# PEER experts of a hybrid decoder step: sample rows gathered like the row blocks, second products summed over four keys

## The chip, the cores and the metric

One core of a Trainium2 chip runs the whole step as one program. The metric is the device time of one execution in microseconds (us); lower is better. The engines are named as in the profile: PE (TensorE matmuls), PEld (its weight loads), DVE (VectorE), ACT (ScalarE), POOL (GpSimd, which issues the indirect DMAs) and SP (the engine that issues most other DMAs).

## The reference, cut to what matters

The step has 1024 prompt rows and 64 sample rows of width 1024. After the mixer sublayer every row goes through PEER: eight heads pick 16 of 16384 experts each, so a row has 128 picks, each with a gate. An expert is a pair of rows (two keys name it) in `expert_u` and `expert_v`.

```python
def block(tb):
    ...
    experts = e1 * N_KEYS + e2
    gate = jax.nn.softmax(top_s, axis=-1)
    ue = expert_u[experts]
    act = jax.nn.gelu(jnp.einsum('thkd,td->thk', ue, tb).astype(F32), approximate=False) * gate
    return jnp.einsum('thk,thkd->td', act.astype(tb.dtype), expert_v[experts])
```

The result is added to the residual, and a final RMSNorm follows.

## The kernel before, in words

The stages follow one another: input projection, SSD heads, RWKV heads, output projection (`output_projection`), picking (`pick_experts`), the spreading of gates (`spread_gates`), and the experts (`run_experts`, line 2787). The change leaves the first three as they are, but for the columns of `mixed` to which they store.

1088 rows are kept. They are split in two parts that are treated differently in `run_experts`:

- **Dense rows**: `DENSE = KEPT - BLOCKS * P` = 704 (the 64 samples and 640 prompt rows), as columns of `h` and `u`. For them all 16384 experts are computed, and the gate, zero for experts not picked, weighs the result. `spread_gates` turns picks into a gate table in DRAM, 64 rows (a group) at a time, each group in 8 batches of 8 rows: 11 groups, 88 batches.
- **Row blocks**: `BLOCKS = 3` blocks of 128 prompt rows, rows on partitions. For pick j of block b an indirect DMA on POOL fetches 128 rows of 4 KB (512 KB) of the first table (`fetch_u`), DVE forms a dot with `rows.u` (`dot_row`, line 3110), ACT takes Gelu of six dots at once, DVE weighs them (`weigh`, line 3115), a second indirect DMA fetches the rows of the second table (`fetch_v`) and DVE adds them with their weight to `rows.h` (`add_row`, line 3123).

`run_experts` goes over 64 periods. In each, g, the dense part handles two values of one key (`SET = 2`). PE makes the first products (`up_products`: 2 keys x 2 chunks of 352 columns x 8 x 3, for every product in full precision is three fp32r matmuls, lines 113 to 115, on a rounded part and a rest) and the second products of the period before (`down_products`: 8 tiles m x 2 chunks x 2 keys x 3): 192 matmuls. ACT rounds weights and activations and takes Gelu; DVE makes the rests (`rest`, line 3086: four of 1024 columns, two of 704), multiplies with the gates (line 3101, two of 704) and adds each of the eight tiles m from PSUM to `h` (`add_units`, line 3129, 704 columns). SP loads two `up` and two `down` weight tiles of 512 KB and 704 KB of gates. Beside this stand six dots and six adds of the row blocks, with 12 gathers of 512 KB.

The order on each engine is written out by hand: `loads` on SP, `fetches` on POOL, `products` on PE, `rounds` on ACT, `vectors` on DVE. An engine takes its instructions in that order, and waits at each for semaphores. There are three buffers each for fetched u rows and v rows (`u_row`, `v_row`), and a fetch waits until DVE has used the buffer. PSUM has two slots for the second products, so tile m waits until tile m - 2 is added.

## Time and profile before

| what | value |
|---|---|
| median of 3 runs | 3923.13 us (3918.64 to 3928.49) |
| time of the profiled execution | 3933.49 us |
| its span on the core | 3931.8 us |
| mean granted TensorE clock | 0.947 of full speed |
| instructions | 64749 |
| PE, DVE, ACT, POOL busy | 91%, 80%, 31%, 35% of the span |
| moved by DMA | 722.81 MB, mean 184 GB/s |

The span is what the profiler saw between the first and the last instruction. Matmuls are pipelined, so a matmul of 322 ns does not occupy PE for 322 ns: the distance between the starts of two neighbours (called pitch below) is what one costs.

### The profile page before, as it was taken

To read this page: it belongs to the slowest core of one execution; us is meant where nothing else is said; L and a number is where in the kernel's file an instruction comes from. 1 tells how busy PE (TensorE), PEld (TensorE's weight loads), DVE (VectorE), ACT (ScalarE), POOL (GpSimd) and SP (SyncE) were. 2 spreads that over 40 slices of the span, in tenths; PEclk is the share of its full clock that TensorE was granted. 3 is DMA by queue.
4 is the path that set the end of the run, shared out by engine and by line. 5 is a ranking of instruction groups with operands and counts; after the bars stand their busy time and mean duration, and the time that the engine had idled before them with its cause. 6 is when DMAs were issued, how large, how long until landed. Compare 5 with 4: busy or idle time off the path is not lost.

```text
span 3931.8 us, 64749 instructions
## 1 busy us (share of the span) xinstructions
PE 3589.7 (91%) x21988; PEld 3328.7 (85%) x21988; DVE 3158.9 (80%) x6167; ACT 1205.8 (31%) x2407; POOL 1371.9 (35%) x1138
## 2 busy tenths in 40 slices
PE   7998848998979998487799999999999999999997
PEld 7997737777769555377799999999999999999996
DVE  7542766667653799999799999999999999999998
ACT  2102434434222222399422222222222222222221
POOL 2120000000000244400355555555555555555552
PEclk9998878889889999699999999999999999999998
DMA  3222220000003001044788888888888988888885
GB/s 118 96 95 95 80 93 26 12 21 12 10 27 126 25 25 37 11 173 211 286 299 297 295 290 292 295 297 296 293 290 286 302 297 293 296 290 294 295 298 178
DMA packets 287394, 722.81 MB, mean 184 GB/s; under 512 B 25928, under 2 KB 136136, under 8 KB 285744
## 3 DMA queue, kind: packets, MB, share of 16 engines
q0 software_dynamic: 117136, 426.42, 32.1%
q1 hardware_dynamic: 170144, 294.96, 21.8%
q8 instruction: 60, 0.98, 0.1%
q14 instruction: 54, 0.44, 0.0%
HBM read 646.99 MB, written 74.30 MB: 183 GB/s over the span
## 4 chain that ended last, share of the span: by engine, by line
PE 48%; DVE 4%; issue 3%; DMA 1%; DVEq 1%; ACT 0%; POOL 0%; ACTq 0%; SPq 0%; POOLq 0%
PE experts_down_ps L113 9%; PE experts_down_ps L114 8%; PE experts_down_ps L115 8%; PE experts_up_ps L113 8%; PE experts_up_ps L114 8%; PE experts_up_ps L115 8%; DVE spread_gate_j L2764 2%; DVEq L2764 0%; DMA stream_u<-in_up_rows,experts_u_at 0%; DMA gates<-spread_spread 0%; DMA stream_h_rest<-in_up 0%; DVE stream_h L3129 0%; DVE stream_h_rows_of L3123 0%; DVEq L2653 0%; ACT spread_gate_j L2719 0%
## 5 line engine op out<-in xcount | busy, mean ns | idle before, releaser
L2923 POOL DMA_INDIRECT stream_u<-in_up_rows,experts_u_at x384 | 540.9, 1409 | 628.3 <-DVE experts_dot L3110 511.5
L113 PE MATMUL experts_down_ps<-experts_act_hi,experts_down_hi 128*128 128x352 f32 x2048 | 676.8, 330 | 8.8 <-DVE experts_down_lo L3086 6.4
L113 PE MATMUL experts_up_ps<-experts_u_hi,experts_up_hi 128*128 128x352 f32 x2048 | 661.6, 323 | 13.1 <-DVE experts_u_lo L3086 6.7
L114 PE MATMUL experts_up_ps<-experts_u_lo,experts_up_hi 128*128 128x352 f32 x2048 | 661.0, 323 | 0.0
L114 PE MATMUL experts_down_ps<-experts_act_lo,experts_down_hi 128*128 128x352 f32 x2048 | 660.7, 323 | 0.0
L115 PE MATMUL experts_up_ps<-experts_u_hi,experts_up_lo 128*128 128x352 f32 x2048 | 660.7, 323 | 0.0
L115 PE MATMUL experts_down_ps<-experts_act_hi,experts_down_lo 128*128 128x352 f32 x2048 | 660.0, 322 | 0.0
L2930 POOL DMA_INDIRECT stream_u<-in_down,experts_v_at x384 | 515.2, 1342 | 242.0 <-issue 113.5
L3110 DVE CUSTOM_DVE_ANT_0 stream_u<-stream_u,stream_u_rows_of 128x1024 f32<-128x1024 f32 x384 | 466.4, 1215 | 83.6 <-DMA stream_u<-in_up_rows,experts_u_at 82.0
L3123 DVE SCALAR_TENSOR_TENSOR stream_h_rows_of<-stream_u,experts_weight,stream_h_rows_of 128x1024 f32<-128x1024 f32 x384 | 497.7, 1296 | 15.0 <-DVE experts_weight L3115 6.8
L3129 DVE TENSOR_TENSOR stream_h<-stream_h,experts_down_ps 128x704 f32<-128x704 f32 x512 | 450.6, 880 | 64.0 <-PE experts_down_ps L115 61.5
L113 PEld LDWEIGHTS experts_down_ps<-experts_act_hi,experts_down_hi 128*128 128x128 f32 x2048 | 385.3, 188 | 34.9 <-DVE stream_h L3129 23.6
L113 PEld LDWEIGHTS experts_up_ps<-experts_u_hi,experts_up_hi 128*128 128x128 f32 x2048 | 386.4, 189 | 13.5 <-DVE experts_up_lo L3086 13.5
L114 PEld LDWEIGHTS experts_up_ps<-experts_u_lo,experts_up_hi 128*128 128x128 f32 x2048 | 386.5, 189 | 0.0
L115 PEld LDWEIGHTS experts_up_ps<-experts_u_hi,experts_up_lo 128*128 128x128 f32 x2048 | 386.3, 189 | 0.0
L114 PEld LDWEIGHTS experts_down_ps<-experts_act_lo,experts_down_hi 128*128 128x128 f32 x2048 | 386.1, 189 | 0.0
L115 PEld LDWEIGHTS experts_down_ps<-experts_act_hi,experts_down_lo 128*128 128x128 f32 x2048 | 385.7, 188 | 0.0
L3028 ACT ACTIVATE experts_down_hi<-stream_u 128x1024 fp32r<-128x1024 f32 x128 | 135.3, 1057 | 707.2 <-PE experts_down_ps L115 707.2
L113 PE MATMUL inp_proj<-inp_u_hi,inp_w_in_hi 128*128 128x368 f32 x648 | 216.9, 335 | 20.7 <-DVE inp_w_in_lo L350 12.3
L2700 PE MATMUL spread_g_ps<-spread_gate_j,spread_hot_i 128*128 128x128 f32 x1408 | 181.2, 282 | 47.9 <-ACT spread_gate_j L2719 47.9
L2700 PEld LDWEIGHTS spread_g_ps<-spread_gate_j,spread_hot_i 128*128 128x128 f32 x1408 | 165.1, 193 | 64.2 <-issue 64.2
L114 PE MATMUL inp_proj<-inp_u_lo,inp_w_in_hi 128*128 128x368 f32 x648 | 215.7, 333 | 0.0
(453 smaller groups left out, 6398.2 us busy)
## 6 DMA issues: line engine op xcount, KB each, us to landing
stream_h_rest<-in_up SPq DMA_DIRECT2D x128, 512.0 KB, 3.9
stream_u<-in_down SPq DMA_DIRECT2D x128, 512.0 KB
gates<-spread_spread SPq DMA_DIRECT2D x11, 4096.0 KB, 11.5
experts_gates<-gates SPq DMA_DIRECT2D x64, 704.0 KB
cols<-inp_done POOLq DMA_DIRECT2D x26, 576.0 KB, 3.8
inp_w_in<-in_w_in SPq DMA_DIRECT2D x27, 512.0 KB, 4.4
pick_w_query<-in_w_query SPq DMA_DIRECT2D x14, 512.0 KB, 3.9
stream_u<-in_up_rows,experts_u_at POOLq DMA_INDIRECT x384
```

Of the source, the lines that this page charges most:

```text
L113: pe.matmul(out, w_hi, x_hi, start=start, stop=False)
L114: pe.matmul(out, w_hi, x_lo, start=False, stop=False)
L115: return pe.matmul(out, w_lo, x_hi, start=False, stop=stop)
L2700: mm = pe.matmul(g_ps[a][:, t, :], hot_i[a][:, t, :], gate_j[a][:, t, :], start=True, stop=True)
L2764: last = dve.tensor_scalar(gate_j[a][:, t, :], iota[:], e2, gate, ALU.is_equal, ALU.mult)
L2923: pool.indirect_dma_start(u_row[b][:], None, up_rows_d, bass.IndirectOffsetOnAxis(ap=u_at[slot][:, b, a:a + 1], axis=0)).then_inc(u_row_lo ...
L2930: pool.indirect_dma_start(v_row[b][:], None, v_table, bass.IndirectOffsetOnAxis(ap=v_at[slot][:, b, a:a + 1], axis=0)).then_inc(v_row_load ...
L3028: act.activation(down_hi[:, e, :], down[e][:], ACT.Copy).then_inc(down_rounded, 1)
L3110: dve.tensor_tensor_reduce(u_row[b][:], u_row[b][:], rows.u[:, b, :], 1.0, 0.0, ALU.mult, ALU.add, dot[slot][:, b, a:a + 1]).then_inc(dott ...
L3123: dve.scalar_tensor_tensor(out=rows.h[:, b, :], in0=v_row[b][:], scalar=weight[slot][:, b, a:a + 1], in1=rows.h[:, b, :], op0=ALU.mult, op ...
L3129: dve.tensor_tensor(row, row, down_ps[m % 2][:, :, 0:DC], ALU.add).then_inc(added, 1)
```

## The change

- The 64 sample rows leave the dense part: `DENSE` is 640, in two chunks of 320 columns. The prompt rows now stand first and the samples last in `h` and `u`.
- The samples become a fourth, half block. Partitions 0 to 63 hold the 64 samples, partitions 64 to 127 the same 64 rows again (a DMA in `spread_gates` copies them). The lower half takes picks 0 to 63, the upper half picks 64 to 127, so one gather of 128 rows serves two picks of every sample, and 64 gathers serve them all: one u fetch and one v fetch per set, into one buffer (`half_row`) that both share. A set now has `FETCHES = 7` u and 7 v fetches. At the end a DMA moves the upper half's sums down and DVE adds them.
- `run_experts` goes over 32 quads of four keys. The second products of a quad are summed over its four keys in PSUM, so `add_units` runs 8 times in a quad where it ran 16 times in two periods. Their weights come from a new array, `down_pieces`, as four pieces of 256 output columns for all four keys (4 KB per partition, 512 KB a piece), in two slots.
- PE's order in a quad: first products of key 0, second products of the quad before, first products of keys 1 to 3. `act_hi` and `act_lo` have four keys and one slot. All orders are written anew.
- `spread_gates` handles 10 groups; several of its tiles share storage with others. The picking turns a fourth block (16 turns where there were 12), and its scores come to DVE in groups of 2, 4 and 3 row tiles where they came in 2, 2 and 5. In the output projection the column chunks are 320, 320 and 448 where they were 352, 352 and 384.

The diff, cut to its core (of the functions in `run_experts` only the new lines stand here):

```diff
-DENSE = KEPT - BLOCKS * P
+DENSE = PROMPT - BLOCKS * P
 DC = DENSE // 2
 DENSE_CHUNKS = ((0, DC), (DC, DC))
+OUT_CHUNKS = (*DENSE_CHUNKS, (DENSE, KEPT - DENSE))
...
+FETCHES = SET * BLOCKS + 1
+HALF_DOT, HALF_ADD = BLOCKS, FETCHES - 1
+QUAD_SIZE = 4
+QUADS = N_KEYS // QUAD_SIZE
+PIECES = 4
+PIECE = D // PIECES
+ROW_BUFFERS = 2 + 2 * BLOCKS + 1
...
+                def down_products(q):
+                    pe.wait_ge(act_split, FROM + q * QUAD_SIZE + QUAD_SIZE)
+                    for m in range(KD):
+                        r, half = divmod(m, 2)
+                        if half == 0:
+                            pe.wait_ge(down_split, FROM + q * PIECES + (r + 1))
+                        pe.wait_ge(added, FROM + q * KD + (m - 1))
                         for c, (lo, n) in enumerate(DENSE_CHUNKS):
+                            for e in range(QUAD_SIZE):
+                                cut = slice(e * PIECE + half * P, e * PIECE + half * P + P)
+                                mm = product(pe, down_ps[m % 2][:, c, 0:n], down_hi[:, r % 2, cut], down_lo[:, r % 2, cut],
+                                             act_hi[:, e, lo:lo + n], act_lo[:, e, lo:lo + n], e == 0, e == QUAD_SIZE - 1)
                         mm.then_inc(down_done, 1)
+                def products(q):
+                    if has(q):
+                        up_products(q, 0)
+                    if has(q - 1):
+                        down_products(q - 1)
+                    if has(q):
+                        for e in range(1, QUAD_SIZE):
+                            up_products(q, e)
+                over_quads(pe, products)
...
+                    a, b = dot_item(i)
+                    if i == HALF_DOT:
+                        if isinstance(g, int) and g < 2:
+                            pool.wait_ge(dotted, FROM + g * (HALF_DOT + 1))
+                        else:
+                            pool.wait_ge(row_added, FROM + g * FETCHES - FETCHES)
+                    else:
+                        pool.wait_ge(dotted, FROM + g * FETCHES + (i - 2 if a == 0 else i - BLOCKS))
                     pool.sem_inc(u_buffer_free, 1)
...
+                def fetches_of_set(g, slot):
+                    this, last, following = has_set(g), has_set(g - 1), has_set(g + 1)
+                    if isinstance(g, int) and g == 0:
+                        list_u(g, slot)
+                        for i in range(BLOCKS + 1):
+                            fetch_u(g, slot, i)
+                    if this:
+                        fetch_u(g, slot, 4)
+                        fetch_u(g, slot, 5)
+                    if last:
+                        fetch_v(g - 1, 1 - slot, 3)
+                    if this:
+                        fetch_u(g, slot, 6)
+                    if last:
+                        fetch_v(g - 1, 1 - slot, 4)
+                        fetch_v(g - 1, 1 - slot, HALF_ADD)
+                        fetch_v(g - 1, 1 - slot, 5)
+                    if following:
                         list_u(g + 1, 1 - slot)
+                        fetch_u(g + 1, 1 - slot, 0)
+                    if this:
+                        list_v(g, slot)
+                        fetch_v(g, slot, 0)
+                    if following:
+                        fetch_u(g + 1, 1 - slot, 1)
+                    if this:
+                        fetch_v(g, slot, 1)
+                    if following:
+                        fetch_u(g + 1, 1 - slot, 2)
+                    if this:
+                        fetch_v(g, slot, 2)
+                    if following:
+                        fetch_u(g + 1, 1 - slot, HALF_DOT)
+                def fetches(q):
+                    fetches_of_set(q * 2, 0)
+                    if has(q):
+                        fetches_of_set(q * 2 + 1, 1)
...
+                def vectors(q):
+                    now, before, following = has(q), has(q - 1), has(q + 1)
+                    def dots(half, i):
+                        if now:
+                            dot_row(q * 2 + half, half, i)
+                    def adds(half, i):
+                        if half == 1 and now:
+                            if i == 0:
+                                weigh(q * 2, 0)
+                            add_row(q * 2, 0, i)
+                        elif half == 0 and before:
+                            if i == 0:
+                                weigh(q * 2 - 1, 1)
+                            add_row(q * 2 - 1, 1, i)
+                    def units(m):
+                        if before:
+                            add_units(q - 1, m)
+                    if before:
+                        gate(q - 1, 3)
+                    dots(0, 0)
+                    if before:
+                        split_act(q - 1, 3)
+                    if now:
+                        split_up(q, 1)
+                    dots(0, 1)
+                    adds(0, 0)
+                    dots(0, 2)
+                    if now:
+                        gate(q, 0)
+                    adds(0, 1)
+                    units(0)
+                    if now:
+                        split_up(q, 2)
+                    dots(0, 3)
+                    units(1)
+                    adds(0, 2)
+                    if before:
+                        split_down(q - 1, 2)
+                    units(2)
+                    dots(0, 4)
+                    adds(0, 3)
+                    units(3)
+                    if before:
+                        split_down(q - 1, 3)
+                    dots(0, 5)
+                    units(4)
+                    adds(0, 4)
+                    dots(0, 6)
+                    units(5)
+                    adds(0, 5)
+                    adds(0, 6)
+                    units(6)
+                    if now:
+                        split_down(q, 0)
+                    dots(1, 0)
+                    units(7)
+                    if now:
+                        split_act(q, 0)
+                    dots(1, 1)
+                    adds(1, 0)
+                    if now:
+                        split_down(q, 1)
+                    dots(1, 2)
+                    adds(1, 1)
+                    if now:
+                        gate(q, 1)
+                    dots(1, 3)
+                    if now:
+                        split_up(q, 3)
+                        split_act(q, 1)
+                    adds(1, 2)
+                    dots(1, 4)
+                    adds(1, 3)
+                    if now:
+                        gate(q, 2)
+                    dots(1, 5)
+                    if following and now:
+                        split_up(q, 4)
+                    if now:
+                        split_act(q, 2)
+                    adds(1, 4)
+                    dots(1, 6)
+                    adds(1, 5)
+                    adds(1, 6)
...
```

## Rows read from the trace of the kernel before

**Rows 1.** Stretches: length, PE, PEld, DVE, ACT, POOL busy us (xcount), clock, DMA share, GB/s.

```profile
2500.00:3700.00 1200.00, 1199.90 (x7441) 1184.00 (x7440) 1114.64 (x1358) 288.83 (x426) 682.68 (x544) 1.00 0.88 294
```

**Rows 2.** Groups of instructions by line and shape, 2500 to 3700 us.

```profile
L3123 DVE SCALAR_TENSOR_TENSOR stream_h_rows_of<-stream_u,experts_weight,stream_h_rows_of 128x1024 f32<-128x1024 f32 x233 | 302.2, 1297 | 7.0 <-DVE experts_weight L3115 4.3
L3110 DVE CUSTOM_DVE_ANT_0 stream_u<-stream_u,stream_u_rows_of 128x1024 f32<-128x1024 f32 x233 | 283.0, 1215 | 46.8 <-DMA stream_u<-in_up_rows,experts_u_at 45.3 <-issue 1.4
L3129 DVE TENSOR_TENSOR stream_h<-stream_h,experts_down_ps 128x704 f32<-128x704 f32 x312 | 274.5, 880 | 31.7 <-PE experts_down_ps L115 31.5 <-issue 0.2
L3086 DVE TENSOR_TENSOR experts_down_lo<-stream_u,experts_down_hi 128x1024 fp32r<-128x1024 f32 x78 | 94.7, 1215 | 0.0
...
L2923 POOL DMA_INDIRECT stream_u<-in_up_rows,experts_u_at x233 | 328.6, 1410 | 382.3 <-DVE experts_dot L3110 311.7 <-issue 35.6 <-POOL experts_v_at L2915 35.0
L2930 POOL DMA_INDIRECT stream_u<-in_down,experts_v_at x233 | 312.6, 1342 | 135.0 <-issue 66.7 <-DVE stream_h_rows_of L3123 34.7 <-POOL experts_u_at L2911 33.5
L2911 POOL COPY experts_u_at<-stream_expert_at 128x6 uint32 x39 | 29.9, 767 | 0.2
L2915 POOL COPY experts_v_at<-stream_expert_at 128x6 uint32 x39 | 14.4, 369 | 0.1
```

**Rows 3.** PE in order of time, 352 columns; lines 1 and 22 of a run.

```profile
3010.25 0.33 PE L113 MATMUL experts_up_ps<-experts_u_hi,experts_up_hi 128*128 128x352 f32 x1
...
3013.61 0.32 PE L113 MATMUL experts_up_ps<-experts_u_hi,experts_up_hi 128*128 128x352 f32 x1
```

**Rows 4.** PE in order of time, 384 columns; lines 1 and 24 of a run.

```profile
1249.97 0.34 PE L113 MATMUL outp_out<-outp_y_hi,outp_w_out_hi 128*128 128x384 f32 x1
...
1253.99 0.33 PE L115 MATMUL outp_out<-outp_y_hi,outp_w_out_lo 128*128 128x384 f32 x1
```

**Rows 5.** Weight loads in order of time, 128-column products of the gate spreading.

```profile
1888.33 1.86 PEld L2700 LDWEIGHTS spread_g_ps<-spread_gate_j,spread_hot_i 128*128 128x128 f32 x16 [0.74 <-issue]
```

**Rows 6.** DVE in order of time, without idle time between them.

```profile
3104.94 1.21 DVE L3086 TENSOR_TENSOR experts_down_lo<-stream_u,experts_down_hi 128x1024 fp32r<-128x1024 f32 x1
3106.08 1.21 DVE L3110 CUSTOM_DVE_ANT_0 stream_u<-stream_u,stream_u_rows_of 128x1024 f32<-128x1024 f32 x1
...
3107.22 1.27 DVE L3123 SCALAR_TENSOR_TENSOR stream_h_rows_of<-stream_u,experts_weight,stream_h_rows_of 128x1024 f32<-128x1024 f32 x1
3108.42 1.21 DVE L3110 CUSTOM_DVE_ANT_0 stream_u<-stream_u,stream_u_rows_of 128x1024 f32<-128x1024 f32 x1
```

**Rows 7.** Readers of outp_out, DVE; min/median/max ns at two widths.

```profile
L2211 DVE TENSOR_TENSOR stream_h<-stream_h,outp_out x16: 514/521/523, 1201.4 to 1275.3; 128x352 f32<-128x352 f32 x8, 128x352 f32 x8
L2211 DVE TENSOR_TENSOR stream_h_rest<-stream_h_rest,outp_out x8: 547/554/555, 1202.3 to 1278.1; 128x384 f32<-128x384 f32 x4, 128x384 f32 x4
```

**Rows 8.** POOL in order of time: two gathers for dots.

```profile
3070.43 1.70 POOL L2923 DMA_INDIRECT stream_u<-in_up_rows,experts_u_at  x1 [0.30 <-issue]
...
3074.36 1.64 POOL L2923 DMA_INDIRECT stream_u<-in_up_rows,experts_u_at  x1 [0.30 <-issue]
```

**Rows 9.** DVE in order of time: the dots that read those two.

```profile
3077.45 1.21 DVE L3110 CUSTOM_DVE_ANT_0 stream_u<-stream_u,stream_u_rows_of 128x1024 f32<-128x1024 f32 x1
...
3083.07 1.23 DVE L3110 CUSTOM_DVE_ANT_0 stream_u<-stream_u,stream_u_rows_of 128x1024 f32<-128x1024 f32 x1 [1.22 <-DMA stream_u<-in_up_rows,experts_u_at]
```

**Rows 10.** A 3 us stretch with all 16 DMA engines at work.

```profile
3084.00:3087.00 3.00, 3.00 (x20) 3.00 (x20) 3.00 (x5) 0.34 (x1) 1.58 (x2) 1.00 1.01 403
```

**Rows 11.** Tile experts_up_ps: first and last start of its products.

```profile
L113 PE MATMUL experts_up_ps<-experts_u_hi,experts_up_hi x2048: 318/322/660, 1897.1 to 3861.2; 128*128 128x352 f32 x187
```

**Rows 12.** Tile experts_down_ps: first and last start of its products.

```profile
L115 PE MATMUL experts_down_ps<-experts_act_hi,experts_down_lo x2048: 317/322/495, 1939.3 to 3901.4; 128*128 128x352 f32 x187
```

**Rows 13.** The first 31 us of the expert stage; columns as in rows 1.

```profile
1897.00:1928.00 31.00, 24.54 (x124) 24.28 (x125) 19.77 (x27) 12.03 (x18) 10.45 (x10) 0.80 0.91 327
```

**Rows 14.** Tile spread_g_ps: first and last start, two records per product.

```profile
L2700 PE MATMUL spread_g_ps<-spread_gate_j,spread_hot_i x1408: 274/275/576, 1663.9 to 1890.1; 128*128 128x128 f32 x176
```

**Rows 15.** ACT in order of time at the end of picking.

```profile
1635.74 2.12 ACT L2443 ACTIVATE pick_by_place<-pick_added_key 128x2304 bf16<-128x2304 bf16 x1 [18.97 <-DVE pick_added_key L2544]
```

577 lines of the change are left out of this document (283 added, 294 removed).

## The prediction

> **What bounds the kernel now.** I read the busy slices first, then the windows of the expert stage, its groups of instructions, and the order of time on PE, DVE and POOL. The expert stage runs from the first product of `experts_up_ps` at 1897.1 us to the last of `experts_down_ps` at 3901.4 us [rows 11, 12]: 2004.3 of 3931.8 us. In its middle PE is busy for 1199.90 of 1200 us at full clock and finishes 7441 matmuls [rows 1]: one in 161.3 ns. So a period of 192 costs 30.96 us, and two periods, the work of one quad, 61.9 us. 64 periods are 1981.4 us; the other 22.9 us are start and end, where 124 matmuls stand in the first 31 us, at a mean clock of 0.80 [rows 13].
>
> The reader is to see that PE's wall is thin. DVE is busy for 1114.64 of 1200 us, 93% [rows 1]. The DMA engines show a share of 0.88 at 294 GB/s [rows 1]. POOL's busy time looks harmless, but a gather costs it 1410 or 1342 ns and then 0.30 us before the next starts [rows 2, 8]. The dots wait 45.3 us for fetched rows in this stretch [rows 2]. So I work out all four engines for a quad.
>
> **PE.** A matmul of 352 columns has a pitch of (3013.61 - 3010.25) / 21 = 160 ns, one of 384 columns (1253.99 - 1249.97) / 23 = 174.8 ns [rows 3, 4]. The slope, 0.46 ns a column, is near one column per cycle of 2.4 GHz (0.42), so 320 columns give 145.2 to 146.7 ns. I take 146.7: 384 of them are 56.3 us, and with the gaps that separate 161.3 from 160 ns, 56.8 us. This holds if the weight load doesn't set the pitch: 16 loads of 128x128 took 1.86 us, 116 ns each [rows 5], so it doesn't. PE alone would give 56.8 us instead of 61.9.
>
> **DVE.** Per quad it has 14 dots and 14 adds (12 and 12 before), 8 rests of 1024 columns, and 16 operations of 640 columns (8 units, 4 gates, 4 rests of activations), where there were 24 of 704. Without idle time the starts stand 1.14 us apart after a rest, 1.14 after a dot and 1.20 after an add [rows 6]. The 880 ns of a unit [rows 2] overlap their neighbour by the same 0.08, so 0.80 at 704 columns. Width costs (554 - 521) / 32 = 1.03 ns a column [rows 7], so 0.734 at 640. Sum: 14 x 1.14 + 14 x 1.20 + 8 x 1.14 + 16 x 0.734 = 53.6, with two weighings 54.0 us. The same sum for before is 28.4 a period with the weighing, where the trace has 1114.64 / 1200 x 30.96 = 28.76; scaled by that, 54.7 us. That the units are halved pays for the four extra row operations. DVE is then 2 us short of PE, against 4.4 us in two periods before.
>
> **POOL.** 28 gathers x (1.376 + 0.30) = 46.9 us, and four lists of indices (two of 767 ns, two of 369 ns [rows 2]), after each of which I add 0.6 us beyond the usual gap: 4.7. Together 51.6 us of issuing in 56.8. Before it was 24 gathers, 44.9 us in 61.9.
>
> **DMA.** A quad moves 28 gathers and 8 weight tiles of 512 KB and 2 x 640 KB of gates: 20.19 MB; two periods moved 18.22 MB, which in 61.9 us is the 294 GB/s of the row. At 56.8 us that is 355 GB/s. If the share of 0.88 were stretched to 1, the engines would give 334 GB/s; but a 3 us stretch with share 1.01 moved 403 GB/s [rows 10], so much of the share is packets that wait for their first byte. I take the engines as able to follow, at a longer latency. The Trainium skill, in "DMA: Bandwidth & Descriptors", section "Specifications", gives about 358 GB/s as the HBM limit of one core. The trace shows more for a short stretch, not for a quad; by the page a quad can't be under 56.4 us, and the sum would be the same, with hardly a reserve.
>
> **What is late next: the gathers.** I laid DVE's new order against PE (0 = first product of key 0; the second products from 7.0 to 35.2, a tile m every 3.52), with the durations above. The dots of the second half then end at 34.7, 37.9, 41.5, 44.6, 48.9, 52.0 and 56.2 us. POOL goes through its list in order: behind the fetch for the sixth v row it must list, and then issue u, v, u, v, u for the next set, each of 1.68 us. It has no pause left there, and the issues of the three u fetches end at 52.3, 56.7 and 60.1. Their dots would start at 57.7, 60.7 and 63.2, that is 5.4, 4.0 and 3.1 us later. Two fetches show what one needs [rows 8, 9]: one whose issue ended at 72.13 was there for a dot at 77.45 (at most 5.3 us), one whose issue ended at 76.00 let the dot start at 83.07 only (7.1 us). With 5.7 us the three stalls sum to 2.6 us, with 7.1 to 4.0. DVE's quad is 54.7 + 2.6 to 4.0 = 57.3 to 58.7 us; I take 57.9, nearer to the short end, since the weight loads are now spread over the quad and no longer come in pairs. In the first half the dots have 10 us and more. PE itself tolerates DVE about 2.7 us behind this plan: tile m needs tile m - 2 added, and the rests of up weights stand 3 us ahead. So a quad is 57.9 us, set by DVE with its waits, PE idling 1.1 us at a time.
>
> **Start and end of the stage.** In the first quad `split_up(0, 1)` stands behind the first dot, and `split_up(0, 3)` behind the dots of the second half. Each waits for a gather round trip (1.7 us of issue and 5.3 to 7.1), and PE runs below full clock after such a pause. I charge 25 us (bounds 15 and 35) on top of 28.2 us for its first products; the last second products are 28.2 us with nothing to overlap, and the end of the chain of activations 5. Stage after: 86.4 + 31 x 57.9 = 1881.3 us, 123.0 less.
>
> **The rest.** Spreading ran 88 batches from 1663.9 to 1890.1 us [rows 14], 2.57 us each; eight go: -20.6 us, and a turn of picks less, -1. The two copies by DMA there are needed 16 batches later or not until the end, so 0; uncovered they would be some 3 us. The four extra turns of the picking fall into the 18.97 us that ACT waits for DVE [rows 15]; without that cover 4 us. The scores' new grouping leaves DVE's operations as they are: 0, bounds -3 and +3. The output projection has the same sum of columns: 0. At the end one block more is squared and scaled (2.4 us) and the halves are joined (0.9), but no adds are left behind the last unit (-3.8) and columns are fewer (-1): -1 to -2 in all, with the turn of picks -2.
>
> Sum: 3933.5 - 123.0 - 20.6 - 2 = 3787.9 for a profiled execution. The profiled one of before lies 10.4 us above the median of 3923.1, so I subtract that: **3777 us**. One us in a quad is 31 us in the total.
>
> **The rivals.**
> - *PE's wall holds* (quad 56.8): the gathers come in 5 us or less and DVE's lag is absorbed. For it: 403 GB/s [rows 10] and evenly spread dots. Against it: 3.1 us of slack for the third fetch. 3777 - 34 = 3743 us.
> - *The DMA engines are the wall* (quad 60.4): 334 GB/s is all that mixed traffic gives, 20.19 MB need 60.4 us. For it: 0.88 at 294 [rows 1]. Against it: rows 10. 3777 + 78 = 3855 us.
> - *POOL is the wall, slower than before.* Its issues stretch where DVE is busy: the two of rows 8 took 1.70 and 1.64 us, not 1.38. With 1.70 for all, 28 x 2.0 + 4.7 = 60.7, and some 4 us a quad in which it waits for dots: 64.7 us, 3988 us. It decides from a quad of 62.6 us on, a mean issue of 1.63 us. Against it: DVE was at 93% already, and the mean over both kinds is 1.376.
> - *The change doesn't do what it says on PE*: the pitch stays at 160 ns with 320 columns. A quad of 61.9 us, 3901 us. Against it: rows 3 to 5.
>
> **How the numbers follow.** Forecast 0.50, PE's wall 0.16, DMA 0.18, POOL 0.08, pitch 0.05; 0.03 for anything else that leaves the time as it is. About 0.3%, 12 us, is what a measurement of this kernel can tell from no change. Faster by more: 0.89; within: 0.03; slower by more: 0.08. The range goes from 3725 (PE's wall with a short start) to 3865 (the DMA wall with 10 us for the start and the picking); pitch, POOL and the rest of 0.16 stay out.
>
> **What would show it.** Right: in the middle of the stage a pitch near 146.7 ns, a quad near 58 us, DVE at 94 to 96%, dots that wait for DMA about 3 us a quad, mostly the first three of an even set, 345 to 350 GB/s, a POOL with almost no idle time but at the first half's dots; ten groups of spreading in 206 us. Wrong: DVE waits for second products (PE's wall), fetches that take 10 us and a share of 1.0 (DMA), indirect issues of 1.6 us and more (POOL), or a start of the stage that costs far more than 25 us.

## The result and the profile after

The changed kernel took 3778.7 us (median of 4 runs, 3777.7 to 3779.7), the kernel before 3924.0 us (median of 4, 3918.6 to 3928.5). The ratio is 0.963, with an interval of 0.9614 to 0.9647. The forecast was 3777 us. Of the six executions of the later kernel e7 one took 5168 us, at a mean granted clock of 0.60, and is not counted in its row.

The sum lies 2 us off, but its terms do not: the picking was 14.4 us over its term and the stage of the experts 23.8 us under it. Together these left the profiled execution (3777.7 us) 10 us under the sum of 3787.9 us. The last step of the forecast closed that gap: it took off 10.4 us, by which the profiled execution of before lay above its median, while the one of after lies 1.0 us below its own. The table compares the two profiled executions (before 3931.8 us of span, after 3776.1).

| part, us | forecast | profiled |
|---|---|---|
| up to the first head of the picking | 0 | -1.8 |
| picking, to the first spread product | 0 (-3 to +3) | +14.4 |
| spreading, to the first product of the experts | -21.6 | -20.1 |
| stage of the experts | -123.0 | -146.8 |
| behind it | -1 | -1.4 |
| sum | -145.6 | -155.7 |

The marks are the first and last starts of three groups of products (columns: count, min/median/max ns, first and last start), of the kernel after. They answer to [rows 11, 12, 14].

```profile
L2712 PE MATMUL spread_g_ps<-stream_h_rest,spread_hot_i x640: 275/275/574, 1676.5 to 1880.1; 128*128 128x128 f32 x160
L113 PE MATMUL experts_up_ps<-experts_u_hi,experts_up_hi x2048: 302/309/636, 1889.6 to 3713.1; 128*128 128x320 f32 x187
L113 PE MATMUL experts_down_ps<-experts_act_hi,experts_down_hi x2048: 302/309/472, 1952.4 to 3746.8; 128*128 128x320 f32 x187
...
L115 PE MATMUL experts_down_ps<-experts_act_hi,experts_down_lo x2048: 302/309/472, 1952.7 to 3747.1; 128*128 128x320 f32 x187
```

The stage takes 3747.1 - 1889.6 = 1857.5 us. From its first second product to its last, 1952.4 to 3747.1, there are 31 quads and then the 192 matmuls of the last one alone (28.2 us): (1794.7 - 28.2) / 31 = 57.0 us a quad. The same formula serves for every kernel below (where 64 matmuls of a quad are left out, with 18.8 for 28.2).

The middle of the stage, 2500 to 3700 us, columns as in [rows 1]:

```profile
2500.00:3700.00 1200.00, 1193.32 (x8085) 1187.11 (x8084) 1150.76 (x1432) 304.60 (x463) 844.74 (x674) 1.00 0.97 353
```

PE is busy for 99.4%, DVE for 95.9%, and the core moves 353 GB/s. DVE's 0.959 x 57.0 = 54.7 us of work in a quad is what the prediction had summed up. The pitch of a matmul of 320 columns is (3005.93 - 2999.19) / 46 = 146.5 ns, in PE's order of time:

```profile
2999.19 0.31 PE L113 MATMUL experts_down_ps<-experts_act_hi,experts_down_hi 128*128 128x320 f32 x1
...
3005.93 0.31 PE L114 MATMUL experts_down_ps<-experts_act_lo,experts_down_hi 128*128 128x320 f32 x1
```

The groups of DVE and POOL in the same stretch show nearly the durations that were taken from [rows 2]. The unit is shorter, 819 ns at 640 columns for 880 at 704, and so are the issues of gathers (1357 for 1410 ns for u, 1310 for 1342 for v):

```profile
L3226 DVE SCALAR_TENSOR_TENSOR stream_h_rows_of<-stream_u,experts_weight,stream_h_rows_of 128x1024 f32<-128x1024 f32 x295 | 374.5, 1281 | 18.8 <-DMA stream_u<-in_down,experts_v_at 7.9 <-DVE experts_weight L3213 3.9 <-issue 3.4
L3209 DVE CUSTOM_DVE_ANT_0 stream_u<-stream_u,stream_u_rows_of 128x1024 f32<-128x1024 f32 x295 | 359.5, 1219 | 13.8 <-DMA stream_u<-in_up_rows,experts_u_at 12.5 <-issue 1.1
L3232 DVE TENSOR_TENSOR stream_h<-stream_h,experts_down_ps 128x640 f32<-128x640 f32 x168 | 137.5, 819 | 14.6 <-PE experts_down_ps L115 13.5 <-issue 0.6
...
L2982 POOL DMA_INDIRECT stream_u<-in_up_rows,experts_u_at x295 | 400.2, 1357 | 199.1 <-DVE experts_dot L3209 84.3 <-issue 81.2 <-POOL experts_u_at L2963 33.6
L2997 POOL DMA_INDIRECT stream_u<-in_down,experts_v_at x295 | 386.4, 1310 | 158.1 <-issue 65.7 <-POOL experts_v_at L2967 37.2 <-DVE experts_dot L3209 28.0
```

The waits of the same stretch (engine, line, releaser: us in total, times, longest):

```profile
DVE stream_h L3232 <- PE experts_down_ps L115: 13.5, 38, 0.4
...
DVE stream_u L3209 <- DMA stream_u<-in_up_rows,experts_u_at: 12.5, 14, 2.2
...
DVE stream_h_rows_of L3226 <- DMA stream_u<-in_down,experts_v_at: 7.9, 20, 0.9
PE experts_down_ps L113 <- DVE stream_h L3232: 4.7, 7, 2.2
```

1200 us hold 21 quads. The dots wait 0.6 us a quad for fetched rows and the adds 0.4; the units wait 0.64 us for products, and PE waits 0.22 us for units. Both engines now run close behind each other, and neither waits long.

### The profile page after: what moved, and what is told of

The parts are those of the page before. It is cut to its first block and busy times, and to the rows that moved or that the text cites. A ratio compares the mean times of both kernels' runs of the same rounds, so it can differ in the third digit from the quotient of the medians.

```text
span 3776.1 us, 64063 instructions
## 1 busy us (share of the span) xinstructions
PE 3400.2 (90%) x21871; PEld 3155.2 (84%) x21871; DVE 3066.7 (81%) x6071; ACT 1169.7 (31%) x2361; POOL 1518.2 (40%) x1267
## 5 line engine op out<-in xcount | busy, mean ns | idle before, releaser
L2982 POOL DMA_INDIRECT stream_u<-in_up_rows,experts_u_at x448 | 601.2, 1342 | 305.1 <-DVE experts_dot L3209 136.8
L113 PE MATMUL experts_up_ps<-experts_u_hi,experts_up_hi 128*128 128x320 f32 x2048 | 635.8, 310 | 28.2 <-DVE experts_up_lo L3180 21.4
L113 PE MATMUL experts_down_ps<-experts_act_hi,experts_down_hi 128*128 128x320 f32 x2048 | 638.7, 312 | 12.5 <-DVE stream_h L3232 7.6
L115 PE MATMUL experts_up_ps<-experts_u_hi,experts_up_lo 128*128 128x320 f32 x2048 | 634.7, 310 | 0.8 <-issue 0.8
L114 PE MATMUL experts_down_ps<-experts_act_lo,experts_down_hi 128*128 128x320 f32 x2048 | 635.0, 310 | 0.2 <-issue 0.2
L115 PE MATMUL experts_down_ps<-experts_act_hi,experts_down_lo 128*128 128x320 f32 x2048 | 634.9, 310 | 0.0
L114 PE MATMUL experts_up_ps<-experts_u_lo,experts_up_hi 128*128 128x320 f32 x2048 | 634.9, 310 | 0.0
L3209 DVE CUSTOM_DVE_ANT_0 stream_u<-stream_u,stream_u_rows_of 128x1024 f32<-128x1024 f32 x448 | 545.8, 1218 | 38.3 <-DMA stream_u<-in_up_rows,experts_u_at 36.7
L3125 ACT ACTIVATE stream_h_rest<-experts_up_ps 128x320 f32<-128x320 f32 x256 | 111.0, 435 | 456.8 <-PE experts_up_ps L115 440.8
L3232 DVE TENSOR_TENSOR stream_h<-stream_h,experts_down_ps 128x640 f32<-128x640 f32 x256 | 209.6, 819 | 33.9 <-PE experts_down_ps L115 32.5
L113 PE MATMUL inp_proj<-inp_u_hi,inp_w_in_hi 128*128 128x368 f32 x648 | 216.4, 334 | 22.5 <-DVE inp_w_in_lo L350 14.1
L115 PE MATMUL inp_proj<-inp_u_hi,inp_w_in_lo 128*128 128x368 f32 x648 | 214.9, 332 | 0.0
```

What stands on the lines that cost most here:

```text
L113: pe.matmul(out, w_hi, x_hi, start=start, stop=False)
L114: pe.matmul(out, w_hi, x_lo, start=False, stop=False)
L115: return pe.matmul(out, w_lo, x_hi, start=False, stop=stop)
L2982: pool.indirect_dma_start((half_row if i == HALF_DOT else u_row[b]), None, up_rows_d, bass.IndirectOffsetOnAxis(ap=u_at[slot][:, col:col + ...
L3125: act.activation(act_v[e % 2][:, lo:lo + n], up_ps[e % 2][c][:, 0:n], ACT.Gelu).then_inc(gelu_ready, 1)
L3209: dve.tensor_tensor_reduce(row, row, rows.u[:, b, :], 1.0, 0.0, ALU.mult, ALU.add, dot[slot][:, col:col + 1]).then_inc(dotted, 1)
```

## The experiments

Two questions: what sets a quad of 57.0 us, and what made the picking 14 us longer. The kernels are numbered e1 to e10.

**e1: POOL's sums one search earlier.** The profile after had shown where the picking lost time. Behind the searches of each of its eight heads DVE has a copy of 9 elements and the pair sums. In the kernel before, the first head starts at 1301.79 us, and in the third head the copy takes 0.18 us:

```profile
1301.79 0.15 DVE L2517 COPY pick_best<-pick_total 128x1 f32<-128x1 f32 x1 [8.05 <-ACT pick_scores L2464]
...
1429.00 0.18 DVE L2542 COPY pick_added_key<-pick_top_key 128x9 bf16<-128x9 bf16 x1
```

In the kernel after, the copy of the third head takes 1.14 us, some 2 us behind six searches (MAX8) of 0.21 us each; in the last head a group of four pair sums takes 4.62 us:

```profile
1299.98 0.15 DVE L2520 COPY pick_best<-pick_total 128x1 f32<-128x1 f32 x1 [1.23 <-ACT pick_scores L2467]
...
1427.80 1.25 DVE L2537 MAX8 pick_top<-pick_rest 128x8 f32<-128x128 f32 x6
...
1431.12 1.14 DVE L2545 COPY pick_added_key<-pick_top_key 128x9 bf16<-128x9 bf16 x1
...
1644.74 4.62 DVE L2558 TENSOR_TENSOR stream_u<-pick_top 128x48 f32<-128x48 f32 x4
```

At the same moments POOL works on bf16 and fp32 tiles in SBUF, in its own order of time:

```profile
1428.34 2.37 POOL L2313 TENSOR_TENSOR pick_sum<-pick_sum 128x1152 bf16<-128x1152 bf16 x1
1430.79 1.43 POOL L2315 TENSOR_TENSOR pick_sum<-pick_sum 128x576 bf16<-128x576 bf16 x1
...
1643.17 6.03 POOL L2358 TENSOR_TENSOR stream_u<-stream_u,picking_mean_square 128x640 f32<-128x640 f32 x4
```

POOL paces itself by DVE's searches. With groups of 2, 4 and 3 tiles instead of 2, 2 and 5, the search it waits for comes some 6 us later in a head (the sums of the third head start 22.5 us into it, where they started 16.0 us into it), and its chain of sums now ends over DVE's copies. The copy ends at 1432.26 and POOL's instruction at 1432.22. The edit, made in both places:

```diff
-                    pool.wait_ge(searches, START + i * 6 + 11)
+                    pool.wait_ge(searches, START + i * 6 + 10)
                     sum_hits(pool, i)
```

> The changed kernel, with one edit in the picking: POOL starts the halving sums of the hits one search earlier in each head (at the first search over the pair sums of the second group of tiles, not at the first search of the third group), so that they end before DVE's copies of the keys. Nothing is left out. Theory A (the collision): the 12.6 us by which the first products of the spreading came later (1676.5 against 1663.9 us) are DVE instructions held up while POOL's sums run: one copy of 9 elements takes 1.14 us instead of 0.18 and the pair sums behind it 0.4 us more, 1.5 us a head, and in the last head 4 us more. Then the first spread products come at 1665 to 1668 us, and the time is 3768 to 3770 us, 0.960 of the kernel before. Theory B (the grouping 2, 4, 3 or the fourth block's turns themselves delay PE and ACT): nothing moves, 1676 us and 3778 us, 0.963.

Measured: 3768.0 us (3757.7 to 3773.6, 5 runs), ratio 0.959 (0.9569 to 0.961). Its DVE, and its first spread product:

```profile
1292.43 0.15 DVE L2520 COPY pick_best<-pick_total 128x1 f32<-128x1 f32 x1 [7.50 <-ACT pick_scores L2467]
...
1423.48 0.19 DVE L2545 COPY pick_added_key<-pick_top_key 128x9 bf16<-128x9 bf16 x1
```

```profile
L2712 PE MATMUL spread_g_ps<-stream_h_rest,spread_hot_i x640: 275/275/575, 1658.3 to 1861.9; 128*128 128x128 f32 x160
```

The copy is back at 0.19 us. Absolute times mislead here, for this execution was already 7.5 us earlier at the first head. Counted from there, the picking takes 1658.3 - 1292.4 = 365.9 us, against 376.5 in the kernel after and 362.1 before. The eight profiles with the unedited order gave 376.2 to 376.5. So 10.6 of the 14.4 us are this collision: theory A, though the first spread product came earlier than forecast. e1 does not remove it everywhere: in its last head the copy still takes 1.40 us, and in the kernel before it took 1.53 us there.

**e2: fewer second products.** Of the three matmuls of each second product, the one with `act_lo` is left out, 64 of 384 a quad.

```diff
-                                mm = product(pe, down_ps[m % 2][:, c, 0:n], down_hi[:, r % 2, cut], down_lo[:, r % 2, cut],
-                                             act_hi[:, e, lo:lo + n], act_lo[:, e, lo:lo + n], e == 0, e == QUAD_SIZE - 1)
+                                pe.matmul(down_ps[m % 2][:, c, 0:n], down_hi[:, r % 2, cut], act_hi[:, e, lo:lo + n], start=e == 0, stop=False)
+                                mm = pe.matmul(down_ps[m % 2][:, c, 0:n], down_lo[:, r % 2, cut], act_hi[:, e, lo:lo + n], start=False, stop=e == QUAD_SIZE - 1)
```

> The changed kernel, but of the three matmuls of each second product the one with the rest of the activations is left out (this part of the result is missing). A quad has 320 matmuls, 46.9 us at a pitch of 146.7 ns, so PE is no longer the bound, while DVE, POOL and DMA do what they did. Theory A (PE was the wall, and DVE with its waits is the next one): the quad falls from 57.0 us to DVE's 54.7 us, or to 57.0 at most if my 2.6 to 4.0 us of waits for gathers had been right; by their measured 1 us, 55 to 56. Theory B (the DMA engines are full): it stays at 56.9 to 57.1 us, 353 GB/s. The Trainium skill's page 'DMA: Bandwidth & Descriptors', section 'Specifications', gives about 358 GB/s as the HBM limit of a core, by which no quad could be under 56.4 us. Theory C (POOL's issues): 51.6 us of issuing and some 2 us of waits, 53 to 54.

Measured: 3748.2 us. Its second products, and 1000 us of its middle:

```profile
L3070 PE MATMUL experts_down_ps<-experts_act_hi,experts_down_hi x2048: 302/309/637, 1953.1 to 3716.8; 128*128 128x320 f32 x187
...
L3071 PE MATMUL experts_down_ps<-experts_act_hi,experts_down_lo x2048: 302/309/472, 1953.3 to 3716.9; 128*128 128x320 f32 x187
```

```profile
2500.00:3500.00 1000.00, 883.91 (x5671) 855.46 (x5670) 965.08 (x1207) 252.44 (x389) 718.70 (x570) 0.97 0.98 359
```

A quad is (3716.9 - 1953.1 - 18.8) / 31 = 56.3 us. With 9.4 us of matmuls gone it gets only 0.7 us shorter, and DVE is busy for 54.3 of it. The next wall stands right behind PE. C falls, A and B stay: 56.3 us is also 359 GB/s.

**e3 and e4: which wall it is.** Both start from e2. e3 narrows DVE's two instructions of the half block to 8 elements, e4 loads an eighth of each weight tile after the first ones. Of both edits one of two places is shown; the add of the half block and the loads of `down` are changed alike.

```diff
-                    dve.tensor_tensor_reduce(row, row, rows.u[:, b, :], 1.0, 0.0, ALU.mult, ALU.add, dot[slot][:, col:col + 1]).then_inc(dotted, 1)
+                    wide = 8 if i == HALF_DOT else D
+                    dve.tensor_tensor_reduce(row[:, 0:wide], row[:, 0:wide], rows.u[:, b, 0:wide], 1.0, 0.0, ALU.mult, ALU.add, dot[slot][:, col:col + 1]).then_inc(dotted, 1)
...
-                    sp.dma_start(up[e % 2], at(up_d, q * QUAD_SIZE + e)).then_inc(up_loaded[e % 2], 16)
+                    sp.dma_start(up[e % 2][:, 0:P], at(up_d, q * QUAD_SIZE + e)[:, 0:P]).then_inc(up_loaded[e % 2], 16)
```

> As the kernel with fewer products, and the dot and the add of the half block work on 8 of 1024 elements (that part of the result is missing); their gathers stay. DVE has 4 x 1.1 = 4.4 us less in a quad. If DVE is the wall behind PE (A), the quad falls from the other kernel's value to 51 to 53 us, where POOL's 51.6 us comes in. If the DMA engines are (B), it stays where the other kernel was, 56.4 to 57 us. If POOL is (C), it stays at 53 to 54.

> As the kernel with fewer products, and the weight tiles of 512 KB are loaded only to an eighth after the first ones (that part of the result is wrong); the gathers and DVE's work stay. A quad moves 16.5 instead of 20.2 MB. If DVE is the wall behind PE (A), the quad stays within 0.5 us of the kernel with fewer products, less the last microsecond of waits for gathers: 54.7 to 55.5. If the DMA engines are (B), it falls by up to 18%, to DVE's 54.7 at least. If POOL is (C), nothing changes.

Measured: e3 3660.1 us, e4 3741.8 us. The same 1000 us of e3, then of e4:

```profile
2500.00:3500.00 1000.00, 918.69 (x5965) 901.51 (x5966) 933.77 (x1264) 267.73 (x410) 752.10 (x594) 0.97 1.00 375
```

```profile
2500.00:3500.00 1000.00, 885.75 (x5653) 864.64 (x5652) 960.64 (x1204) 251.61 (x388) 717.70 (x567) 0.95 0.87 293
```

e3's quad is 53.7 us (second products from 1944.9 to 3629.4 us), e4's 56.4 us (1944.5 to 3710.5). Less DVE work shortens the quad by 2.6 us, and 18% less DMA traffic (293 GB/s) does nothing. So DVE with its waits is the wall behind PE, and the DMA engines are not. e3 moved 375 GB/s over 1000 us, so the 358 GB/s that the Trainium skill gives ("DMA: Bandwidth & Descriptors", "Specifications") did not bind this core; the measurement decides. e3 fell less than forecast. DVE waits 2.9 us a quad for gathers there, at a DMA share of 1.00. POOL is nearly full there as well: beside its issues and the gaps of 0.30 us behind them it waited 28 of 1000 us for DVE, 1.5 us a quad, against 5.3 in e2.

```profile
L2997 POOL DMA_INDIRECT stream_u<-in_down,experts_v_at x260 | 361.4, 1390 | 105.6 <-issue 65.1 <-POOL experts_v_at L2967 32.8 <-DVE stream_h_rows_of L3228 4.1
L2982 POOL DMA_INDIRECT stream_u<-in_up_rows,experts_u_at x260 | 337.8, 1299 | 142.1 <-issue 95.7 <-POOL experts_u_at L2963 25.7 <-DVE experts_dot L3210 20.7
```

The 53.7 us also lie in the range of theory C. Whether the latency, the load of the DMA engines or POOL's issuing sets the floor of e3 was not tested.

**e8: more DVE work.** An additional instruction beside each unit.

```diff
+                    spare_of_bank, again = down_ps[m % 2][:, :, DC:BANK], slice(0, BANK - DC)
+                    dve.tensor_tensor(spare_of_bank, u_lo[:, m, :].rearrange("p (c n) -> p c n", c=2)[:, :, again], down_ps[m % 2][:, :, again], ALU.add)
                     dve.tensor_tensor(row, row, down_ps[m % 2][:, :, 0:DC], ALU.add).then_inc(added, 1)
```

> The changed kernel with eight additional DVE instructions in a quad, one beside each unit (384 columns, one operand from PSUM, result unused): by the width slope of 1.03 ns a column 0.734 - 256 x 0.00103 = 0.47 us each, 3.8 us a quad. It stands for a part of what the sum over four keys saves DVE (eight units, 5.9 us). Theory A (DVE with its waits stands at 56.3 us, as the kernel with fewer products showed, 0.7 us under PE's wall): the quad becomes 56.3 + 3.8 = 60.1 us, 3778.7 + 31 x 3.1 = 3875 us. Theory B (PE's wall has more room under it, at least the 2.3 us that DVE is idle in a quad of 57.0): 58.5 us, 3825 us. Then what the second products' sum over four keys was worth can be read: 56.3 + 5.9 = 62.2 us without it in A.

Measured: 3846.3 us. The group of the added instruction, and the same 1000 us:

```profile
L3233 DVE TENSOR_TENSOR experts_down_ps<-experts_u_lo,experts_down_ps 128x384 f32<-128x384 f32 x133 | 73.4, 552 | 0.7 <-PE experts_down_ps L115 0.7
```

```profile
2500.00:3500.00 1000.00, 963.42 (x6446) 955.58 (x6445) 975.57 (x1278) 240.64 (x372) 622.33 (x539) 0.99 0.94 339
```

The instruction takes 552 ns, 0.47 behind the usual overlap, as the slope of [rows 7] says. The quad is (3815.2 - 1940.9 - 28.2) / 31 = 59.6 us, 2.6 us more for 3.8 us of work: nearer to A's 60.1 than to B's 58.5. DVE is busy for 58.1 of it, and its waits have shrunk from 2.0 us (e2) to 1.5. Eight more units would be 5.9 us of work: 54.3 + 5.9 + 1.5 to 2.0 = 61.7 to 62.2 us a quad, as long as two periods before. That is worked out, not run. By this estimate the rest of the change would have gained nothing in this stage without the sum over four keys.

**e10: less DVE work, all matmuls.** The edit of e3 on the changed kernel.

> The changed kernel, but the dot and the add of the half block work on 8 of 1024 elements (that part of the result is missing); all matmuls and gathers stay. DVE has 4.4 us less in a quad. Theory A (PE's wall, 384 matmuls at its own pitch): the quad falls from 57.0 us by no more than the 0.2 to 0.3 us in which PE waited for units, 56.7 to 56.8 us. Theory B (the forecast: DVE with its waits sets the quad): it falls by more than 0.5 us, towards 384 x 146.7 = 56.3.

Measured: 3748.1 us. Its second products and its middle, and the same 1000 us of the changed kernel below them:

```profile
L113 PE MATMUL experts_down_ps<-experts_act_hi,experts_down_hi x2048: 307/309/417, 1944.3 to 3717.1; 128*128 128x320 f32 x187
...
L115 PE MATMUL experts_down_ps<-experts_act_hi,experts_down_lo x2048: 302/309/309, 1944.7 to 3717.4; 128*128 128x320 f32 x187
```

```profile
2500.00:3500.00 1000.00, 998.28 (x6805) 997.85 (x6805) 901.76 (x1206) 254.16 (x388) 655.58 (x567) 1.00 0.97 358
```

```profile
2500.00:3500.00 1000.00, 993.61 (x6730) 988.33 (x6728) 957.94 (x1192) 255.47 (x389) 701.43 (x562) 1.00 0.97 354
```

The quad is (3717.4 - 1944.3 - 28.2) / 31 = 56.3 us, which is 384 matmuls of 146.5 ns and nothing else. B's row came, not A's: PE's own wall stands at 56.3, and the changed kernel stays 0.7 us above it because of DVE. With the other's work cut, each engine takes 56.3 us (e10, e2); together they take 57.0. e2 and e10 are one execution each. By the same formula the quad was 56.9 to 57.0 us in e5, e6 and e9 and 57.2 to 57.3 in e1 and e7, so the 0.7 us are more than this scatter.

**e6: another order in quad 0.** The prediction put the slow start down to rests of up weights that stand behind dots. The kernel after shows just that: between its first product and its first second product PE stands twice, 21.4 us in all, for such a rest.

```profile
1905.83 0.63 PE L113 MATMUL experts_up_ps<-experts_u_hi,experts_up_hi 128*128 128x320 f32 x1 [6.99 <-DVE experts_up_lo L3180]
...
1936.28 0.64 PE L113 MATMUL experts_up_ps<-experts_u_hi,experts_up_hi 128*128 128x320 f32 x1 [14.43 <-DVE experts_up_lo L3180]
```

e6 moves the rests ahead, on DVE and on ACT, in quad 0 alone.

```diff
+                    if isinstance(q, int) and q == 0:
+                        split_up(q, 1)
+                        dots(0, 0)
+                        gate(q, 0)
+                        split_up(q, 2)
+                        split_act(q, 0)
+                        dots(0, 1)
+                        dots(0, 2)
+                        gate(q, 1)
+                        split_up(q, 3)
...
+                        return
```

> The changed kernel with another order in quad 0 alone: on DVE the rests of the up weights and the gates stand ahead of the dots, on ACT the rounding of up tiles 3 and 4 ahead of the Gelu of the dots. Nothing is left out. In the changed kernel 62.8 us lie between the first product of the stage and its first second product, of which 35.2 us are matmuls: 27.6 us are lost, close to the 25 us of the forecast. Theory A (the step of the forecast: the rests wait in line behind dots, and these for the first gathers): 45 to 52 us, and the stage is 11 to 17 us shorter, 3762 to 3768 us, a ratio of 0.959 to 0.960. Theory B (the row work of quad 0 itself is the bound: 21 gathers of 1.65 us on POOL from 1895 us on, and a round trip, end at 1937 us at the earliest): the first second product comes earlier, but its units stand behind the dots and adds of quad 0, and the gain is given back in quad 1: under 4 us in the total, 3775 to 3780 us.

Measured: 3778.2 us (3768.9 to 3791.5, 4 runs), ratio 0.9625 (0.9603 to 0.9647), no gain. The first second product comes 65.5 us behind the first product of the stage (1944.5 and 1879.0), not 45 to 52. DVE and PE around it:

```profile
1939.10 2.48 DVE L3242 SCALAR_TENSOR_TENSOR stream_h_rows_of<-stream_u,experts_weight,stream_h_rows_of 128x1024 f32<-128x1024 f32 x2
1941.50 0.86 DVE L3212 TENSOR_TENSOR stream_h_rest<-stream_h_rest,experts_gates 128x640 f32<-128x640 f32 x1
```

```profile
1944.46 0.63 PE L113 MATMUL experts_down_ps<-experts_act_hi,experts_down_hi 128*128 128x320 f32 x1 [25.03 <-DVE experts_act_lo L3196]
```

PE waited only 2.7 us for a rest of up weights, had its first products done at 1919.4 us and then stood 25.0 us. What it waits for is the rest of key 3's activations; the gate before it stands at the head of quad 1's list on DVE, behind all dots and adds of quad 0, of which the last ends at 1941.6. In that row work DVE itself waited 18.5 us for gathers. So the wait of the forecast was there, and taking it away moved the loss to the next thing that stands behind the row work of quad 0: B's cause, though the early second product of B did not come. e6 left the gate of key 3 where it was. Whether an order with that gate ahead too starts earlier, and keeps what it gains, no run shows.

**e5, e7 and e9: the changed kernel again, and versions that may beat it.** e5 is the changed kernel. e7 has e6's order and, beside e1's edit in the loop over the heads, POOL's work in the last head moved further; e9 has the picking edits alone:

```diff
                 i = PEER_HEADS - 2
                 for s in range(2):
-                    pool.wait_ge(searches, START + i * 6 + (7 + 2 * s))
+                    pool.wait_ge(searches, START + i * 6 + (7 + s))
                     weigh_hits(pool, i, s)
-                pool.wait_ge(searches, START + i * 6 + 11)
                 sum_hits(pool, i)
...
                 for k in range(KD):
-                    if k == KD // 2:
+                    if k == KD // 2 + 2:
                         pool.wait_ge(searches, START + PEER_HEADS * 6)
```

> The changed kernel itself, as a measure on the same chip for the kernels beside it. Its ratio was 0.963 (0.9614 to 0.9647). Theory: 0.961 to 0.965 again, first spread product near 1676 us, and 62.8 us from the first product of the stage to its first second product.

> The changed kernel with the order in quad 0 of the kernel before this one, and with POOL's work in the picking moved: the halving sums one search earlier in each head (as in the first experiment, which took 10.6 us off the way from the second head to the first spread product), and in the last head everything as early as it can be, with six of eight scalings of u before the last search. Nothing is left out. If both edits act where they stand: 3778.7 - 10.6 - 4 for the last head - 14 for the start of the stage = 3750 us (3745 to 3757), a ratio of 0.954 to 0.957. If the start of the stage gives back its gain (B): 3762 to 3766, 0.959. If the last head's collision only moves to other instructions of DVE, 4 us more.

> The changed kernel with only the moves of POOL's work in the picking that the kernel with both edits had. Nothing is left out. In seven profiles with the changed kernel's picking the way from the first head to the first spread product took 376.3 to 376.5 us, with the sums one search earlier 365.9, with these moves 360.4. Theory A (the collision costs what is seen there, and the stage of the experts doesn't depend on it): 360 to 361 us again, a stage of 1857 to 1860 us, and a time of 3765 us (the runs before gave 3748 to 3780, since the stages ahead of the picking vary by 20 us among executions), a ratio of 0.957 to 0.960. Theory B (an earlier picking lengthens the stage of the experts, as 1866.7 and 1867.8 us in the two profiles with it might say, against 1856.6 to 1859.3 in the three without): a stage of 1866 to 1868 us again.

Measured:

| kernel | us (range, runs) | ratio to before | first head to spread | stage |
|---|---|---|---|---|
| e5 | 3783.5 (3777.2 to 3786.7, 4) | 0.9622 (0.9603 to 0.9641) | 376.3 | 1856.6 |
| e7 | 3765.5 (3748.3 to 3780.5, 5) | 0.9578 (0.9551 to 0.9604) | 360.4 | 1867.8 |
| e9 | 3758.2 (3752.7 to 3771.0, 5) | 0.9577 (0.9557 to 0.9597) | 359.9 | 1854.4 |

e5's first spread product came at 1686.2 us, 10 us later than in the first profile of the same kernel, with the same 376.3 us of picking: the stages ahead of it were late. The marks of e9:

```profile
1296.72 0.15 DVE L2519 COPY pick_best<-pick_total 128x1 f32<-128x1 f32 x1 [7.50 <-ACT pick_scores L2466]
```

```profile
L2711 PE MATMUL spread_g_ps<-stream_h_rest,spread_hot_i x640: 275/275/574, 1656.6 to 1860.1; 128*128 128x128 f32 x160
L113 PE MATMUL experts_up_ps<-experts_u_hi,experts_up_hi x2048: 303/309/636, 1869.5 to 3688.9; 128*128 128x320 f32 x187
L115 PE MATMUL experts_down_ps<-experts_act_hi,experts_down_lo x2048: 302/309/472, 1932.2 to 3723.9; 128*128 128x320 f32 x187
```

e9 has the lowest median of these kernels, 0.9577 against 0.963 for the changed kernel; the intervals of e1, e7 and e9 overlap, so among these three no order is shown. e7 adds nothing to e9, as e6 would have it. The stages of e7 and e1 had been 9 to 10 us longer than the others, which looked like a cost of the earlier picking; e9 has the picking of e7 and a stage of 1854.4 us, so the longer stage does not follow from it. Why those two profiles had the longer waits for gathers (15 and 20 us in 1000, against 9 to 12) is open.

## Why the prediction was right, point by point

- **PE.** Right. 146.5 ns (forecast 146.7), 56.3 us for 384 of them. The 0.5 us of gaps on top are not PE's own: e10 has none.
- **DVE.** Right. 54.7 us of work a quad, summed from durations of before.
- **DMA.** Right. 353 GB/s at a share of 0.97, and e4 shows that the engines don't bind. The rival of 60.4 us is out, e3's 375 GB/s rules it out.
- **POOL.** Right. Gathers of 1357 and 1310 ns, below the 1.63 us from which it would have decided. It waited 139.5 us in 1200 for DVE, 6.6 us a quad, so its own work was 50.4 us (51.6 forecast).
- **The gathers' stalls. This term failed.** The forecast had 2.6 to 4.0 us a quad, and the dots waited 0.6. These are the issues on POOL of the three fetches in question, and on DVE the last dot of the quad, two adds, a gate and the three dots that read those rows:

```profile
2739.68 1.77 POOL L2982 DMA_INDIRECT stream_u<-in_up_rows,experts_u_at  x1 [0.89 <-POOL experts_u_at L2963]
...
2743.95 1.95 POOL L2982 DMA_INDIRECT stream_u<-in_up_rows,experts_u_at  x1 [0.30 <-issue]
...
2747.71 0.94 POOL L2982 DMA_INDIRECT stream_u<-in_up_rows,experts_u_at  x1 [0.30 <-issue]
```

```profile
2743.88 1.21 DVE L3209 CUSTOM_DVE_ANT_0 stream_u<-stream_u,stream_u_rows_of 128x1024 f32<-128x1024 f32 x1
...
2745.31 2.48 DVE L3226 SCALAR_TENSOR_TENSOR stream_h_rows_of<-stream_u,experts_weight,stream_h_rows_of 128x1024 f32<-128x1024 f32 x2 [0.21 <-DMA stream_u<-in_down,experts_v_at]
2747.70 0.86 DVE L3196 TENSOR_TENSOR stream_h_rest<-stream_h_rest,experts_gates 128x640 f32<-128x640 f32 x1
2748.49 1.21 DVE L3209 CUSTOM_DVE_ANT_0 stream_u<-stream_u,stream_u_rows_of 128x1024 f32<-128x1024 f32 x1
...
2751.64 1.22 DVE L3209 CUSTOM_DVE_ANT_0 stream_u<-stream_u,stream_u_rows_of 128x1024 f32<-128x1024 f32 x1
...
2754.68 1.23 DVE L3209 CUSTOM_DVE_ANT_0 stream_u<-stream_u,stream_u_rows_of 128x1024 f32<-128x1024 f32 x1 [0.22 <-DMA stream_u<-in_up_rows,experts_u_at]
```

From the end of an issue to its dot there are 7.0, 5.7 and 6.0 us, and only the last waits, 0.22 us. The plan had 5.4, 4.0 and 3.1 us. The issues came about where the plan had them: counted from the end of the quad's last dot (2743.88 + 1.14), they end 3.6 us before it and 0.9 and 3.6 us behind it, where the plan had 3.9 before, 0.5 and 3.9 behind. The dots came later: 3.5, 6.6 and 9.7 us behind that end, not 1.5, 4.5 and 7.0. In the 22 quads whose last gate lies between 2463 and 3660 us the first of them starts 3.2 to 4.0 us behind it, and in six one of the three waits for its row.

The plan had placed these dots too early, by its own durations. It lets the last dot end at 56.2 and the first of the next set start at 57.7, but by the order in `vectors` two adds (1.20 each) and a gate (0.73) stand between them: 59.3, and then 62.4 and 64.9 for the next two. With that the three fetches have 7.0, 5.7 and 4.8 us, and the two latencies of the forecast, 5.7 and 7.1 us, give some 0.9 and 2.4 us of stalls instead of 2.6 and 4.0. The latency is not refuted (the dot that waited had 6.0 us); the place of the dots was wrong.
- **A quad as the larger of two.** The prediction took the later engine, 57.9 us, and the rival of PE's wall took the other, 56.8. Each engine with the other's work cut takes 56.3 us, and together they take 57.0, so the rival's quad was the nearer one, and the PE idle of 1.1 us at a time did not come. Two near walls cost 0.7 us more than either; that each engine's late moments stop the other is what the waits show (0.64 us a quad of DVE for products, 0.22 of PE for units). The 0.7 us are 22 us of the total. The quad was 0.9 us shorter than forecast, 28 us of the total.
- **Start and end.** 62.8 us up to the first second product and 28.2 for the last ones are 91.0 us, where 86.4 was forecast. 27.6 us were lost ahead of the first second product (25 forecast). The wait was the one forecast: 21.4 us for rests of up weights behind dots. The other 6.2 us go with PE's pace, at a mean granted clock of 0.81 from 1889 to 1953 us. That wait is not all that holds the start, though: without it the loss stays (e6).
- **Spreading and tail.** Right: -20.1 and -1.4 us.
- **Picking. This step failed.** "The scores' new grouping leaves DVE's operations as they are: 0, bounds -3 and +3" counted DVE's instructions and not what POOL does at those moments. The 14.4 us are 0.9 in the first head, 8.7 in the next six and 4.8 in the last. e1 took back 7.3 and 3.3 of the latter two: the collision. It left 0.9, 1.4 and 1.5, whose causes are not shown. The Trainium skill ("SBUF — State Buffer", "SBUF: two separate sides") says that a GpSimd instruction and a DVE instruction lock each other out for a whole instruction where that of DVE is in a 2-port mode, or has two SBUF inputs while GpSimd's reads SBUF. The rows agree: the copy and pair sums were held, while the searches (MAX8) under the same POOL instructions kept their 0.21 us. The rule was at hand and no sentence of the prediction used it.
- **Four turns of the picking** cost nothing, as forecast: ACT's wait at the end of picking is 24.84 us in the kernel after, where it was 18.97 [rows 15], so the extra turns used none of it up.

The two failures had opposite signs and left some 10 us between them, and the 10.4 us taken off for the profiled execution of before happened to cover these. That the total was met within 2 us is luck. The range would have been met with either failure alone.

## What to carry to other kernels

When work is regrouped on one engine, look up what another engine does at the moments where its instructions now fall, above all where that other engine paces itself by a semaphore of the first. When an order is laid out over a period, carry it over the end: what stands behind the last item of one period also stands ahead of the first item of the next. Where two engines had walls of 56.3 us each, the period was 0.7 us longer than either, and taking work off one of them gave back no more than that. At the start of the stage, moving one kind of waiting work ahead gained nothing, for the next instruction behind the same row work then held PE as long: look for everything that stands behind the slow chain before moving one part of it.

## What was not expected of the hardware

- The same unchanged stages ahead of the picking end at different times: in twelve profiles the first head starts between 1288.4 and 1310.0 us. In the stretch from 640 to 1000 us the granted clock was 0.84 in the latest of them and 0.89 in the two earliest; between these the order is not strict (0.85 at 1296.7 us, 0.87 at 1292.4). So times of the picking had to be counted from its own first instruction, and a total of one execution says little about 10 us.
- A copy of 9 elements that takes 0.18 us alone took 1.14 us beside POOL, and four pair sums took 4.62 us instead of the 0.55 of e9.
- One core took in 375 GB/s over 1000 us, with nearly three quarters of the bytes in gathers of 4 KB rows (e3).
